# Gathering the first two expert tiles inside the routing block of a mixture-of-experts encoder

## The chip, the cores and the metric

The kernel runs on one core of a Trainium2 chip. Its time is the device time of one execution in microseconds (us), given as the median of several executions. A core has these engines: TensorE (PE, with its weight loads PEld), VectorE (DVE), ScalarE (ACT), GpSimd (POOL) and SyncE (SP). Each takes its instructions in order from its own sequencer (PEq, DVEq, ACTq, POOLq, SPq in the rows), and they meet through semaphores.

## The reference, cut to what matters

The program is one encoder layer on two sequences of 1024 tokens with 1024 features: a layer norm, a mixer (attention and a gated linear recurrence), a second norm, and then the part that the change touches, a mixture of 16 experts with two experts per token.

```python
def hier_moe(h, ...):
    xt = h.reshape(B * S, D)
    g_onehot = one_hot(argmax(xt @ router_wg + router_bg), 4)         # one of 4 groups
    e_logits_sel = einsum('tge,tg->te', xt @ router_we + router_be, g_onehot)
    top_v, top_i = top_k(e_logits_sel, 2)                             # two of its 4 experts
    top_w = softmax(top_v) * g_sel_prob
    gate = ...                                                        # (token, 16), two entries not zero
    for e in range(16):
        hid = silu(xt @ exp_w1[e]) * (xt @ exp_w3[e])                 # 1024 -> 256
        y = y + gate[:, e] * (hid @ exp_w2[e])                        # 256 -> 1024
```

The result is added to the normed input and normed once more. 2048 tokens with two experts each make 4096 pairs of token and expert, and only those are computed.

## The kernel before, in words

`build` runs six stages one after the other: `project_xy`, `qkv_lru`, `attend`, `route`, `experts` and `combine`. Each stage is a block of five programs, one per engine, with semaphores of its own. At a stage's end each engine runs a DRAIN (the row of the block's own line) and all engines meet; then POOL clears the stage's semaphores (`semaphores`, L193) and all engines drain and meet a second time. Only then does an engine start on the next stage. A context of semaphores that closes costs one such clearing and meeting.

`route` (L1725) sorts the pairs. It gives each expert a run of slots, in tiles of 128 slots, 48 tiles at most. It builds one-hot matrices: `lanes` (L1799) is a table of 128 x 32 bf16 numbers per partition, 8 KB, which ACT fills (L1869) and DVE compares with each pair's lane (L1955). 32 accumulating matmuls (L2002) then yield, for each slot, the token's number and gate. DVE turns that into row numbers, `found` (L1980 to L1983), copies them to `lists` (L1984), makes the gates (L1985 to L1987), and that is its last work of the stage. POOL makes constants at the stage's start and nothing after them. SP loads the weights of experts 0 and 1, and ACT makes the high part of expert 0's weights (L1875).

`experts` (L2006) works on tiles of 128 pairs. All products are of float32 values in three passes, high x high, high x low and low x high, so each weight has a low part, raw minus high. POOL gathers a tile's 128 rows of 4 KB from `h1_dram` into `xg[u]` by an indirect DMA (`ahead`, L2171), from a column of 128 row numbers in `ix[u]` that DVE copies out of `lists` (`index`, L2319). PE transposes the rows (`turn`, L2211), ACT makes their high part (L2291), DVE their low part (L2344), PE multiplies (`up`, L108 to L110), ACT and DVE make `hid` (L2285, L2338), PE multiplies with the second matrix (`down`), ACT scales by the gate (L2298), and POOL adds the tile's rows into `sum_dram` by an indirect DMA with an add (L2187). `run_tiles` writes out this order for every engine, with rows gathered three tiles ahead.

An expert's low parts are made by two engines. Of the four parts of the first matrix DVE makes three and POOL one (L2092, part 3); of the two parts of the second DVE makes one and POOL one (L2099). All are 128 x 1024 subtractions with both inputs in SBUF. For expert 0 this stands at the stage's start. DVE's program there begins:

```python
            index(0, 0)
            index(1, 1)
            split_first(0)
            split_rest(0)
            run_tiles(dve, skip, ahead, split_first, up, turn, skip, turn_hid, split_rest)
```

and POOL's begins:

```python
            ahead(0, 0)
            ahead(1, 1)
            split_rest(0)
            last = run_tiles(pool, skip, ahead, None, skip, skip, down, skip, split_rest)
```

PE's `up` waits for both engines' low parts of the first matrix and for the low part of the rows. SP waits for all low parts of an expert before it loads the expert after next over it (L2159, then L1720 to L1722), and only after it has issued that load does it tell ACT that the next expert's weights are ready (`w_ready`, L2155), which ACT needs before it makes their high part (L2264), still ahead of the first tile's silu (L2285).

Of the kernel before, what the change touches and what calls it, by code (L numbers as in the profile page):

```python
# [26 lines left out]
BF16 = mybir.dt.bfloat16  # L27
# [7 lines left out]
P = 128  # L35
D = 1024
# [76 lines left out]
def build(nc, x, ln_in_g, ln_in_b, w_in, conv_w, conv_b, lru_wa, lru_ba, lru_wx, lru_bx, lru_lambda,  # L113
# [13 lines left out]
    with ExitStack() as whole:  # L127
# [44 lines left out]
        with ExitStack() as kept:  # L172
            sb = lambda n, s, d=F32: kept.enter_context(nc.sbuf_tensor(n, s, d))

            up_w = [sb(n, [P, 2, KD, 2 * DE], d) for n, d in (("up_raw", F32), ("up_hi", F32R), ("up_lo", F32R))]
            down_w = [sb(n, [P, 2, KE, D], d) for n, d in (("down_raw", F32), ("down_hi", F32R), ("down_lo", F32R))]
            route(nc, ident, logits, gates, *tables, exp_w1, exp_w3, exp_w2, up_w, down_w)
            experts(nc, exp_w1, exp_w3, exp_w2, up_w, down_w, ident, gates, *tables, h1_dram, sum_dram)
        combine(nc, ln2_g[0], ln2_b[0], sum_dram, out)

# [1541 lines left out]

def route(nc, ident, logits, gates, lists, tile_expert, split_at, pair_live, last_tile,  # L1725
          exp_w1, exp_w3, exp_w2, up_w, down_w):

# [3 lines left out]
    with ExitStack() as ctx:  # L1733
# [62 lines left out]
        vals = sb("vals", [P, VALS, PAIRS], BF16)  # L1796
        part_i = sb("part_i", [P, 2, PAIRS], I32)
        part = sb("part", [P, 2, PAIRS], BF16)
        lanes = sb("lanes", [P, P, PAIRS], BF16)  # L1799
        tiles = sb("tiles", [P, MT, PAIRS], BF16)  # L1800
        hot_lane = sb("hot_lane", [P, P, PAIRS], BF16)
        hot_tile = sb("hot_tile", [P, MT, PAIRS], BF16)
# [25 lines left out]
        @block.gpsimd  # L1828
        def _(pool):
            link = Chain(pool, pool_link)  # L1830
            for j in range(G):
                pool.memset(order[:, :, j], float(G - j)).then_inc(made, 1)
            pool.memset(ones[:], 1.0).then_inc(made, 1)
            pool.memset(busy[:], 0.0).then_inc(zeroed, 1)
            link(pool.memset(tri_f[:], 0.0))

            link(pool.affine_select(out=tri_f[:], in_=tri_f[:], compare_op=ALU.is_gt, fill=-1.0, base=0,
                                    pattern=[[1, P]], channel_multiplier=-1))
            pool.tensor_copy(tri[:], tri_f[:]).then_inc(made, 1)
            link(pool.memset(from_first[:], 1.0))  # L1840
            pool.memset(from_first[:, :, 0], 0.0).then_inc(made, 1)
            link(pool.iota(thr_i[:], [[P, NT]], base=0, channel_multiplier=0))
            pool.tensor_copy(thr[:], thr_i[:]).then_inc(made, 1)
            link(pool.iota(spare_i[:], [[1, 1]], base=T + 1, channel_multiplier=1))
            pool.tensor_copy(spare[:], spare_i[:]).then_inc(made, 1)
            link(pool.iota(lane_i[:], [[1, P]], base=0, channel_multiplier=0))
            pool.tensor_copy(lane_f[:], lane_i[:]).then_inc(made, 1)
            link(pool.iota(tile_i[:], [[1, MT]], base=0, channel_multiplier=0))
            pool.tensor_copy(tile_f[:], tile_i[:]).then_inc(made, 1)
            link(pool.iota(row_i[:], [[0, NT]], base=1, channel_multiplier=1))  # L1850
            for c in range(2):
                half = slice(c * NT, (c + 1) * NT)
                pool.tensor_copy(vals[:, 0, half], tile_i[:, 0:NT]).then_inc(vals_done, 1)
                pool.tensor_copy(vals[:, 1, half], row_i[:]).then_inc(vals_done, 1)

        @block.sync
        def _(sp):
# [6 lines left out]
        def _(act):  # L1864
# [1 line left out]
            act.activation(ge[:], gd[:], ACT.Exp).then_inc(ge_done, 1)  # L1866

            act.wait_ge(made, G + 7)
            act.activation(lanes[:], lane_f[:].unsqueeze(2).broadcast_to([P, P, PAIRS]), ACT.Copy).then_inc(spread, 1)  # L1869
            act.wait_ge(gap_done, 1)  # L1870
            act.activation(x2[:], gap[:], ACT.Exp).then_inc(x2_done, 1)
            act.activation(tiles[:], tile_f[:].unsqueeze(2).broadcast_to([P, MT, PAIRS]), ACT.Copy).then_inc(spread, 1)
# [6 lines left out]
        def _(dve):  # L1879
# [101 lines left out]
            link(dve.scalar_tensor_tensor(number[:], list_ps[:, 0], float(P), found[:], ALU.mult, ALU.add))  # L1981
            link(dve.tensor_scalar(found[:], number[:], 0.5, spare[:], ALU.is_lt, ALU.mult))
            link(dve.scalar_tensor_tensor(found[:], number[:], -1.0, found[:], ALU.add, ALU.add))  # L1983
            link(dve.tensor_copy(lists[:, 0:MT], found[:]))  # L1984
            link(dve.tensor_copy(gates[:], list_ps[:, 4]))  # L1985
            link(dve.tensor_tensor(gates[:], gates[:], list_ps[:, 3], ALU.add))
# [17 lines left out]

def experts(nc, exp_w1, exp_w3, exp_w2, up_w, down_w, ident, gates, lists, tile_expert, split_at, pair_live, last_tile,  # L2006
            h1_dram, sum_dram):

# [5 lines left out]
    with ExitStack() as ctx:  # L2016
# [8 lines left out]
        DOWN_POOL = 1  # L2025
        up_raw, up_hi, up_lo = up_w
        down_raw, down_hi, down_lo = down_w
        ix = [sb(f"ix{u}", [P, 1], U32) for u in range(2)]
        xg = [sb(f"xg{u}", [P, D]) for u in range(2)]
        xt_hi = [sb(f"xt_hi{u}", [P, KD, P], F32R) for u in range(2)]  # L2030
        xt_lo = [sb(f"xt_lo{u}", [P, KD, P], F32R) for u in range(2)]
        sg = sb("sg", [P, DE])
# [9 lines left out]
        y_ps = [ps(f"y_ps{c}", [P, 512]) for c in range(2)]  # L2042

        go = sem("go")
        ix_done = sem("index_ready")
        x_in = [sem(f"rows_gathered{u}") for u in range(2)]
        w_in = [sem(f"weights_loaded{b}") for b in range(2)]
        w_ready = sem("raw_weights_ready")
        up_hi_made = sem("up_hi_made")
# [116 lines left out]
        def _(pool):  # L2166
            def ahead(j, u):

                pool.wait_ge(ix_done, j + 1)
                pool.nop(nofuse=True)  # L2170
                pool.indirect_dma_start(xg[u][:], None, h1_dram, bass.IndirectOffsetOnAxis(ix[u][:, 0:1], 0))\  # L2171
                    .then_inc(x_in[u], 16)

            def split_rest(e):
# [12 lines left out]
                pool.indirect_dma_start(sum_dram, bass.IndirectOffsetOnAxis(sx[u][:, 0:1], 0), yt[u][:], None,  # L2187
                                        compute_op=ALU.add).then_inc(y_added, 16)

            ahead(0, 0)  # L2190
            ahead(1, 1)
            split_rest(0)
            last = run_tiles(pool, skip, ahead, None, skip, skip, down, skip, split_rest)
            pool.wait_ge(y_added, 16 * last + 16)
# [113 lines left out]
        def _(dve):  # L2308
# [44 lines left out]
                dve.nop(nofuse=True)  # L2353
                dve.tensor_copy(sx[u][:], lists[:, bass.ds(j, 1)]).then_inc(gate_done, 1)

            index(0, 0)
            index(1, 1)
            split_first(0)
            split_rest(0)
            run_tiles(dve, skip, ahead, split_first, up, turn, skip, turn_hid, split_rest)  # L2360
# [232 lines left out]
```

## Time and profile before

| | us |
|---|---|
| median of 3 runs | 1680.79 (1680.5 to 1683.96) |
| the profiled execution | 1685.38 |
| its span, first to last instruction | 1683.6 |
| routing | 1143.0 to 1177.4 of the span |
| experts | 1178.4 to 1625.1 |
| combine | 1626.0 to 1683.6 |

Over the whole span PE is busy 89%, DVE 65%, ACT 54% and POOL 29%, and the mean granted clock of TensorE is 0.946 of full speed. Busy time says how long an engine had an instruction in execution, not that the instruction got on: one that is held up counts as busy too. An indirect DMA on POOL counts as busy while POOL writes its descriptors, and the data moves after that.

### The profile page before, as it was taken

How to read it: one execution, taken by the hardware profiler on the slowest of the kernel's cores; microseconds unless marked ns; L12 is line 12 of the kernel's file. 1: busy time of each engine (PE TensorE's matmuls, PEld its weight loads, DVE VectorE, ACT ScalarE, POOL GpSimd, SP SyncE). 2: the span in 40 equal slices, each digit the busy share in tenths (PEclk: the TensorE clock that was granted, in tenths of full speed). 3: DMA queues.
4: the chain of work that ended last, by engine and by line, in shares of the span. 5: the costliest groups of instructions: out<-in, count | busy, mean ns of one | idle time of the engine just before them, and what ended most of it. 6: DMA issues, size and time to landing. Idle time of an engine off the chain costs nothing. (4 is left out here: it accounts for less than half of the span.)

```text
span 1683.6 us, 29356 instructions
## 1 busy us (share of the span) xinstructions
PE 1505.2 (89%) x8921; PEld 1274.0 (76%) x8923; DVE 1101.9 (65%) x2057; ACT 904.2 (54%) x1505; POOL 496.3 (29%) x345
## 2 busy tenths in 40 slices
PE   5999989999858999999999999996799999999940
PEld 5999967777647888888888888872677788777820
DVE  7787539999968776777777777666553433444238
ACT  3444447878757555555555555532555444556323
POOL 1212125565510111111111111110445443545218
PEclk9999999999969999999999999995899999999965
DMA  8855543344242111112111111124688677796466
GB/s 275 305 211 206 180 152 132 144 168 170 100 159 69 58 57 56 61 64 71 61 57 56 56 56 57 45 95 168 227 258 256 173 219 193 217 269 159 111 185 266
DMA packets 118771, 245.02 MB, mean 146 GB/s; under 512 B 18082, under 2 KB 71330, under 8 KB 118692
## 3 DMA queue, kind: packets, MB, share of 16 engines
q1 hardware_dynamic: 88752, 156.44, 26.6%
q0 software_dynamic: 12528, 45.62, 11.5%
q10 hardware_dynamic: 17412, 41.96, 6.5%
q8 instruction: 44, 0.72, 0.2%
q14 instruction: 35, 0.29, 0.1%
HBM read 149.61 MB, written 94.37 MB: 145 GB/s over the span
## 5 line engine op out<-in xcount | busy, mean ns | idle before, releaser
L1562 DVE TENSOR_TENSOR d_probs_t_lo<-d_pt_ps,d_probs_t_hi 128x512 fp32r<-128x512 f32 x256 | 164.2, 683 | 103.4 <-ACT d_probs_t_hi L1483 102.5
L1483 ACT ACTIVATE d_probs_t_hi<-d_pt_ps 128x512 fp32r<-128x512 f32 x256 | 139.2, 596 | 152.6 <-PE d_pt_ps L1339 146.1
L1705 POOL TENSOR_TENSOR d_h_tile<-d_s_tile,d_ln_g_b 128x512 f32<-128x512 f32 x30 | 38.5, 1282 | 577.5 <-ACT d_s_tile L1501 546.7
L1540 DVE TENSOR_REDUCE d_neg_max<-d_s_ps 128x1 f32<-128x1024 f32 x128 | 155.4, 1214 | 2.7 <-PE d_s_ps L1328 2.7
L108 PE MATMUL acc<-k_hi,wl_hi 128*128 128x256 f32 x512 | 146.2, 286 | 4.4 <-DVE k_lo L518 4.4
L108 PE MATMUL e_a_ps<-up_hi,e_xt_hi 128*128 x336 | 138.7, 413 | 10.5 <-issue 6.1
L110 PE MATMUL acc<-k_hi,wl_lo 128*128 128x256 f32 x512 | 145.4, 284 | 0.0
L109 PE MATMUL acc<-k_lo,wl_hi 128*128 128x256 f32 x512 | 145.3, 284 | 0.0
L1466 ACT ACTIVATE d_probs<-d_s_ps,d_neg_max 128x1024 f32<-128x1024 f32 x128 | 143.3, 1119 | 3.6 <-DVE d_neg_max L1540 3.6
L1357 PE MATMUL d_ot_ps<-d_probs_t_hi,d_v_split 128*128 128x256 f32 x512 | 129.9, 292 | 8.8 <-DVE d_probs_t_lo L1562 6.6
L1339 PE MATMUL d_pt_ps<-ident,d_probs 128*128 128x128 f32 x1024 | 134.0, 274 | 3.3 <-ACT d_probs L1466 3.2
L109 PE MATMUL e_a_ps<-up_lo,e_xt_hi 128*128 x336 | 134.7, 401 | 0.0
L110 PE MATMUL e_a_ps<-up_hi,e_xt_lo 128*128 x336 | 134.3, 400 | 0.0
L1339 PEld LDWEIGHTS d_pt_ps<-ident,d_probs 128*128 128x128 f32 x1024 | 117.7, 141 | 13.2 <-ACT d_probs L1466 5.3
L1357 PE MATMUL d_ot_ps<-d_probs_t_lo,d_v_split 128*128 128x256 f32 x512 | 125.0, 282 | 0.0
L1327 PE MATMUL d_s_ps<-k_hi,d_q_tile 128*128 128x512 f32 (+1 forms) x256 | 113.3, 442 | 4.6 <-DMA d_q_tile<-q_dram 4.6
L2171 POOL DMA_INDIRECT e_xg<-h_dram,e_ix x45 | 45.1, 1003 | 228.7 <-ACT e_yt L2298 130.1
L1357 PEld LDWEIGHTS d_ot_ps<-d_probs_t_hi,d_v_split 128*128 128x128 f32 x512 | 97.2, 190 | 17.5 <-issue 17.5
L1328 PE MATMUL d_s_ps<-k_lo,d_q_tile 128*128 128x512 f32 (+1 forms) x256 | 102.4, 400 | 0.0
L108 PEld LDWEIGHTS acc<-k_hi,wl_hi 128*128 128x128 f32 x512 | 98.1, 192 | 5.0 <-DVE k_lo L518 4.9
L108 PE MATMUL d_m_ps<-d_wo_hi,d_m_hi 128*128 128x512 f32 x240 | 99.4, 414 | 0.0
L109 PEld LDWEIGHTS acc<-k_lo,wl_hi 128*128 128x128 f32 x512 | 98.0, 191 | 0.0
(380 smaller groups left out, 4041.6 us busy)
## 6 DMA issues: line engine op xcount, KB each, us to landing
up_raw<-in_exp_w SPq DMA_DIRECT2D x32, 1024.0 KB, 10.4
down_raw<-in_exp_w SPq DMA_DIRECT2D x16, 1024.0 KB, 12.9
h_dram<-v_all ACTq DMA_DIRECT2D x16, 512.0 KB, 3.4
ht_hi_dram<-k_hi ACTq DMA_DIRECT2D x8, 1024.0 KB, 4.3
ht_lo_dram<-k_lo ACTq DMA_DIRECT2D x8, 1024.0 KB, 6.6
q_dram<-wq_raw ACTq DMA_DIRECT2D x16, 512.0 KB, 3.0
d_q_tile<-q_dram SPq DMA_DIRECT2D x16, 512.0 KB, 3.9
d_h_tile<-h_dram SPq DMA_DIRECT2D x16, 512.0 KB, 3.2
```

Source lines behind the costliest of these rows:

```text
L108: pe.matmul(out, lhs[0], rhs[0], start=first, stop=False)
L109: pe.matmul(out, lhs[0], rhs[1], start=False, stop=False)
L110: return pe.matmul(out, lhs[1], rhs[0], start=False, stop=last)
L1327: pe.matmul(out, q_t[u][:, h, :], k_hi[:, h // GQ, keys], start=True, stop=False)
L1328: last = pe.matmul(out, q_t[u][:, h, :], k_lo[:, h // GQ, keys], start=False, stop=True)
L1339: last = pe.transpose(pt_ps[c][:, j, :], pr[h % 2][:, k * P:(k + 1) * P], ident[:])
L1357: last = pe.matmul(ot_ps[:, 0:2 * P], vs[:, s * TPS + k, h // GQ].rearrange("p c d -> p (c d)"), part[:, k].rearrange("p e t -> p (e t)"), ...
L1466: act.activation(pr[h % 2][:], s_ps[h % 2][:], ACT.Exp, bias=nm[:, u, h:h + 1], accum_out=rsum[:, u, h:h + 1]).then_inc(p_done, 1)
L1483: act.activation(pt_hi[:, c * HALF:(c + 1) * HALF, h % 2], pt_ps[c][:], ACT.Copy).then_inc(pth_done[c], 1)
L1540: dve.tensor_reduce(nm[:, u, h:h + 1], s_ps[h % 2][:], AX, ALU.max, negate=True).then_inc(nm_done, 1)
L1562: dve.tensor_tensor(pt_lo[:, part, h % 2], pt_ps[c][:], pt_hi[:, part, h % 2].bitcast(F32), ALU.subtract)\
L2171: pool.indirect_dma_start(xg[u][:], None, h1_dram, bass.IndirectOffsetOnAxis(ix[u][:, 0:1], 0))\
```

## The change

The two columns of row numbers and the two buffers of rows are now made in `build`, ahead of both stages, with the three semaphores that go with them, in a context of semaphores of their own (`g_`) around `route` and `experts`. The table `lanes` no longer has memory of its own; it lies in the memory of the two row buffers, which is 8 KB per partition as well. DVE copies the first two tiles' numbers straight from `found`, between L1983 and L1984, and POOL issues the first two gathers at the end of its program in `route`. In `experts` the two `index` calls of DVE and the two `ahead` calls of POOL at the start are gone. The gathers of later tiles are as before.

```diff
--- before.py
+++ after.py
@@ -174,8 +174,17 @@
 
             up_w = [sb(n, [P, 2, KD, 2 * DE], d) for n, d in (("up_raw", F32), ("up_hi", F32R), ("up_lo", F32R))]
             down_w = [sb(n, [P, 2, KE, D], d) for n, d in (("down_raw", F32), ("down_hi", F32R), ("down_lo", F32R))]
-            route(nc, ident, logits, gates, *tables, exp_w1, exp_w3, exp_w2, up_w, down_w)
-            experts(nc, exp_w1, exp_w3, exp_w2, up_w, down_w, ident, gates, *tables, h1_dram, sum_dram)
+            ix = [sb(f"e_ix{u}", [P, 1], U32) for u in range(2)]
+            xg_both = sb("e_xg", [P, 2, D])
+            xg = [xg_both[:, u] for u in range(2)]
+            with semaphores(nc, "g_") as sem:
+
+                ix_done = sem("index_ready")
+                x_in = [sem(f"rows_gathered{u}") for u in range(2)]
+                route(nc, ident, logits, gates, *tables, exp_w1, exp_w3, exp_w2, up_w, down_w,
+                      h1_dram, ix, xg_both, ix_done, x_in)
+                experts(nc, exp_w1, exp_w3, exp_w2, up_w, down_w, ident, gates, *tables, h1_dram, sum_dram,
+                        ix, xg, ix_done, x_in)
         combine(nc, ln2_g[0], ln2_b[0], sum_dram, out)
 
 
@@ -1723,7 +1732,7 @@
 
 
 def route(nc, ident, logits, gates, lists, tile_expert, split_at, pair_live, last_tile,
-          exp_w1, exp_w3, exp_w2, up_w, down_w):
+          exp_w1, exp_w3, exp_w2, up_w, down_w, h1_dram, ix, xg_both, ix_done, x_in):
 
 
 
@@ -1796,7 +1805,8 @@
         vals = sb("vals", [P, VALS, PAIRS], BF16)
         part_i = sb("part_i", [P, 2, PAIRS], I32)
         part = sb("part", [P, 2, PAIRS], BF16)
-        lanes = sb("lanes", [P, P, PAIRS], BF16)
+
+        lanes = xg_both[:].rearrange("p u d -> p (u d)").bitcast(BF16).rearrange("p (l i) -> p l i", l=P)
         tiles = sb("tiles", [P, MT, PAIRS], BF16)
         hot_lane = sb("hot_lane", [P, P, PAIRS], BF16)
         hot_tile = sb("hot_tile", [P, MT, PAIRS], BF16)
@@ -1852,6 +1862,10 @@
                 half = slice(c * NT, (c + 1) * NT)
                 pool.tensor_copy(vals[:, 0, half], tile_i[:, 0:NT]).then_inc(vals_done, 1)
                 pool.tensor_copy(vals[:, 1, half], row_i[:]).then_inc(vals_done, 1)
+            for u in range(2):
+                pool.wait_ge(ix_done, u + 1)
+                pool.indirect_dma_start(xg_both[:, u], None, h1_dram, bass.IndirectOffsetOnAxis(ix[u][:, 0:1], 0))\
+                    .then_inc(x_in[u], 16)
 
         @block.sync
         def _(sp):
@@ -1866,7 +1880,7 @@
             act.activation(ge[:], gd[:], ACT.Exp).then_inc(ge_done, 1)
 
             act.wait_ge(made, G + 7)
-            act.activation(lanes[:], lane_f[:].unsqueeze(2).broadcast_to([P, P, PAIRS]), ACT.Copy).then_inc(spread, 1)
+            act.activation(lanes, lane_f[:].unsqueeze(2).broadcast_to([P, P, PAIRS]), ACT.Copy).then_inc(spread, 1)
             act.wait_ge(gap_done, 1)
             act.activation(x2[:], gap[:], ACT.Exp).then_inc(x2_done, 1)
             act.activation(tiles[:], tile_f[:].unsqueeze(2).broadcast_to([P, MT, PAIRS]), ACT.Copy).then_inc(spread, 1)
@@ -1981,6 +1995,8 @@
             link(dve.scalar_tensor_tensor(number[:], list_ps[:, 0], float(P), found[:], ALU.mult, ALU.add))
             link(dve.tensor_scalar(found[:], number[:], 0.5, spare[:], ALU.is_lt, ALU.mult))
             link(dve.scalar_tensor_tensor(found[:], number[:], -1.0, found[:], ALU.add, ALU.add))
+            for u in range(2):
+                dve.tensor_copy(ix[u][:], found[:, u:u + 1]).then_inc(ix_done, 1)
             link(dve.tensor_copy(lists[:, 0:MT], found[:]))
             link(dve.tensor_copy(gates[:], list_ps[:, 4]))
             link(dve.tensor_tensor(gates[:], gates[:], list_ps[:, 3], ALU.add))
@@ -2004,7 +2020,7 @@
 
 
 def experts(nc, exp_w1, exp_w3, exp_w2, up_w, down_w, ident, gates, lists, tile_expert, split_at, pair_live, last_tile,
-            h1_dram, sum_dram):
+            h1_dram, sum_dram, ix, xg, ix_done, x_in):
 
 
 
@@ -2025,8 +2041,6 @@
         DOWN_POOL = 1
         up_raw, up_hi, up_lo = up_w
         down_raw, down_hi, down_lo = down_w
-        ix = [sb(f"ix{u}", [P, 1], U32) for u in range(2)]
-        xg = [sb(f"xg{u}", [P, D]) for u in range(2)]
         xt_hi = [sb(f"xt_hi{u}", [P, KD, P], F32R) for u in range(2)]
         xt_lo = [sb(f"xt_lo{u}", [P, KD, P], F32R) for u in range(2)]
         sg = sb("sg", [P, DE])
@@ -2042,8 +2056,6 @@
         y_ps = [ps(f"y_ps{c}", [P, 512]) for c in range(2)]
 
         go = sem("go")
-        ix_done = sem("index_ready")
-        x_in = [sem(f"rows_gathered{u}") for u in range(2)]
         w_in = [sem(f"weights_loaded{b}") for b in range(2)]
         w_ready = sem("raw_weights_ready")
         up_hi_made = sem("up_hi_made")
@@ -2168,7 +2180,7 @@
 
                 pool.wait_ge(ix_done, j + 1)
                 pool.nop(nofuse=True)
-                pool.indirect_dma_start(xg[u][:], None, h1_dram, bass.IndirectOffsetOnAxis(ix[u][:, 0:1], 0))\
+                pool.indirect_dma_start(xg[u], None, h1_dram, bass.IndirectOffsetOnAxis(ix[u][:, 0:1], 0))\
                     .then_inc(x_in[u], 16)
 
             def split_rest(e):
@@ -2187,8 +2199,6 @@
                 pool.indirect_dma_start(sum_dram, bass.IndirectOffsetOnAxis(sx[u][:, 0:1], 0), yt[u][:], None,
                                         compute_op=ALU.add).then_inc(y_added, 16)
 
-            ahead(0, 0)
-            ahead(1, 1)
             split_rest(0)
             last = run_tiles(pool, skip, ahead, None, skip, skip, down, skip, split_rest)
             pool.wait_ge(y_added, 16 * last + 16)
@@ -2353,8 +2363,6 @@
                 dve.nop(nofuse=True)
                 dve.tensor_copy(sx[u][:], lists[:, bass.ds(j, 1)]).then_inc(gate_done, 1)
 
-            index(0, 0)
-            index(1, 1)
             split_first(0)
             split_rest(0)
             run_tiles(dve, skip, ahead, split_first, up, turn, skip, turn_hid, split_rest)
```

## Rows read from the trace of the kernel before

**Rows 1.** Busy time of each engine by stretch, all times in us.

```profile
core 0: us, PE busy (x) PEld busy (x) DVE busy (x) ACT busy (x) POOL busy (x), PEclk, DMA share, GB/s
1176.00:1185.00 9.00, 0.35 (x2) 0.35 (x3) 6.03 (x12) 0.00 (x0) 4.62 (x3) 0.50 0.27 76
1188.00:1191.00 3.00, 3.00 (x9) 2.35 (x8) 0.04 (x1) 0.02 (x1) 1.20 (x2) 0.52 0.36 102
1191.00:1195.00 4.00, 4.00 (x20) 3.22 (x19) 2.64 (x3) 3.98 (x5) 0.00 (x0) 1.00 1.06 376
1216.00:1616.00 400.00, 382.35 (x1814) 308.29 (x1812) 158.56 (x333) 200.48 (x320) 177.22 (x109) 0.99 0.74 203
```

**Rows 2.** Timeline of DVE at the boundary: start, us, instruction, [idle before].

```profile
1176.29 0.21 DVE L1983 SCALAR_TENSOR_TENSOR r_found<-r_number,r_found 128x48 f32<-128x48 f32 x1
1176.53 0.19 DVE L1984 CAST lists<-r_found 128x48 uint32<-128x48 f32 x1
1177.23 0.20 DVE L1987 TENSOR_TENSOR gates<-gates,list_ps 128x48 f32<-128x48 f32 x1
1178.95 0.21 DVE L2319 COPY e_ix<-lists 128x1 uint32<-128x1 uint32 x2 [1.51 <-ACTq L2254]
1179.10 3.50 DVE L2092 TENSOR_TENSOR up_lo<-up_raw,up_hi 128x1024 fp32r<-128x1024 f32 x3
1182.51 1.22 DVE L2099 TENSOR_TENSOR down_lo<-down_raw,down_hi 128x1024 fp32r<-128x1024 f32 x1
1186.43 0.69 DVE L2344 TENSOR_TENSOR e_xt_lo<-e_t_ps,e_xt_hi 128x512 fp32r<-128x512 f32 x1 [2.71 <-ACT e_xt_hi L2291]
```

**Rows 3.** Timeline of POOL at the start of the experts.

```profile
1180.07 1.31 POOL L2171 DMA_INDIRECT e_xg<-h_dram,e_ix  x1 [32.32 <-DVE e_ix L2319]
1181.68 1.74 POOL L2171 DMA_INDIRECT e_xg<-h_dram,e_ix  x1 [0.30 <-issue]
1183.43 2.50 POOL L2092 TENSOR_TENSOR up_lo<-up_raw,up_hi 128x1024 fp32r<-128x1024 f32 x1
1185.89 2.35 POOL L2099 TENSOR_TENSOR down_lo<-down_raw,down_hi 128x1024 fp32r<-128x1024 f32 x1
```

**Rows 4.** Timelines of PE, SP and ACT in the first tile.

```profile
1184.65 1.97 PE L2211 MATMUL e_t_ps<-ident,e_xg 128*128 128x128 f32 x8 [9.24 <-DMA e_xg<-h_dram,e_ix]
1187.44 0.79 PE L108 MATMUL e_a_ps<-up_hi,e_xt_hi 128*128 x1 [0.82 <-DVE e_xt_lo L2344]
1188.48 0.39 SPq L1720 DMA_DIRECT2D up_raw<-in_exp_w  x1
1190.98 3.90 ACT L2264 ACTIVATE up_hi<-up_raw  x4 [3.72 <-SPq L2155]
1194.90 1.28 ACT L2285 ACT_TABLE_LOAD   x1
```

**Rows 5.** All gathers and scatters: count, shortest/median/longest ns, first and last start.

```profile
L2171 POOL DMA_INDIRECT e_xg<-h_dram,e_ix x45: 936/980/1737, 1180.1 to 1606.0; - x45
L2187 POOL DMA_INDIRECT sum_dram<-e_yt,e_sx x42: 1572/1593/2605, 1209.3 to 1614.8; - x42
```

**Rows 6.** Meeting of the engines at the end of routing (ns, start in us).

```profile
L1733 DVEq DRAIN  x1: 10/10/10, 1177.7 to 1177.7; - x1
L193 ACTq EVENT_SEMAPHORE  x1: 17/17/17, 1178.4 to 1178.4; - x1
```

**Rows 7.** The end of the experts on POOL, and the meetings after it.

```profile
1614.78 1.57 POOL L2187 DMA_INDIRECT sum_dram<-e_yt,e_sx  x1 [5.11 <-DMA sum_dram<-e_yt,e_sx]
L2195 POOLq EVENT_SEMAPHORE  x1: 17/17/17, 1620.7 to 1620.7; - x1
L2016 POOLq DRAIN  x1: 4030/4030/4030, 1621.1 to 1621.1; - x1
L2016 SPq EVENT_SEMAPHORE  x1: 17/17/17, 1625.2 to 1625.2; - x1
L193 SPq EVENT_SEMAPHORE  x1: 17/17/17, 1625.9 to 1625.9; - x1
```

**Rows 8.** Splits of two later experts, timelines of POOL and DVE.

```profile
1240.24 2.73 POOL L2092 TENSOR_TENSOR up_lo<-up_raw,up_hi  x1
1240.32 6.10 DVE L2099 TENSOR_TENSOR down_lo<-down_raw,down_hi  x1 [2.01 <-ACT down_hi L2273]
1242.59 2.74 POOL L2099 TENSOR_TENSOR down_lo<-down_raw,down_hi  x1
...
1413.07 1.23 DVE L2099 TENSOR_TENSOR down_lo<-down_raw,down_hi  x1 [1.60 <-ACT down_hi L2273]
1413.09 3.45 POOL L2092 TENSOR_TENSOR up_lo<-up_raw,up_hi  x1
```

## The prediction

> **What bounds the kernel now.** I read the busy time by stretch first. From 1216 to 1616 PE is busy 382.35 of 400 us at full clock [rows 1]: the stage of the experts runs at the pace of PE, in a fixed order, so whatever delays the first tile's products is not made up later, and whatever brings them forward is kept. From 1176 to 1185 PE is busy 0.35 of 9 us: a hole between two stages, and the change works in it. The timelines of DVE, POOL and PE then show what fills the hole. The row numbers are ready at 1176.50 (L1983), DVE's last result is done at 1177.43, the engines meet, and DVE's first instruction of the next stage starts at 1178.95 [rows 2]. POOL issues the two gathers from 1180.07 to 1183.42, and only then does its two subtractions, to 1188.24 [rows 3]. DVE does its four subtractions from 1179.10 to 1183.73, while POOL writes descriptors [rows 2, 3]. The first rows arrive at 1184.65, PE turns them, DVE's low part starts at 1186.43, and the first product starts at 1187.44, 1.01 us after that [rows 2, 4]. So the wait that ends last before the first product is the one for the gathered rows; the subtractions are done beneath it. The question is what ends last once the rows come early.
>
> **The gathers move.** The two copies of row numbers take 0.21 us [rows 2] and go where L1984 was, at 1176.53; DVE's tail then ends at 1177.64, which costs nothing while POOL is later. From the copies' start to the first gather's was 1180.07 - 1178.95 = 1.12 us, so POOL starts at 1176.53 + 1.12 = 1177.65. A gather takes 0.98 us where nothing slows it [rows 5] (the first two took 1.31 and 1.74 beside DVE's subtractions), with 0.30 between two [rows 3]: the second is issued by 1177.65 + 0.98 + 0.30 + 0.98 = 1179.91. The first gather's rows reached PE 3.27 us after its issue ended (1184.65 - 1181.38). The first tile's rows are thus there at 1181.9, 2.7 us earlier, and the second tile's at about 1183.2, or 1183.3 as the two transfers overlap more.
>
> **What the move puts into POOL's queue.** POOL cannot leave the routing block before its DRAIN is over, and everybody waits for POOL there. The trace has one DRAIN of POOL behind indirect DMAs, at the end of the experts. There the last scatter had landed at 1620.7, and the DRAIN still took 4.03 us from 1621.1 [rows 7]. It is no ordinary empty drain (DVE's took 0.01 us [rows 6]), so it has to do with the DMAs. Bounds: it could cost nothing and let POOL go at 1179.9; it could wait for the landing and then take 4.03 us more, to 1187.3. Between them I take that it waits for the landing and does something for each DMA issued since the last DRAIN: 45 + 42 = 87 of them [rows 5] at 4.03 / 87 = 0.046 us, so 0.1 us for two. POOL is then free at 1183.3 + 0.1 = 1183.4, where DVE was free at 1177.7 [rows 6]. The meeting and clearing take 1178.4 - 1177.7 = 0.7 us [rows 6], so the experts' stage starts at 1184.1 in place of 1178.4: 5.7 us late. The rows are there by then; the gain of 2.7 us is behind another wait.
>
> **What the late start uncovers.** DVE's first instruction came 0.55 us after the start of the stage, with five semaphore increments in front (1178.95 against 1178.4). It now is a subtraction, at 1184.65. POOL no longer has two gathers ahead of its subtractions, has fewer instructions in front than DVE, and starts them at about 1184.5. So for the first time all six subtractions of expert 0 want to run at once. Later experts show what happens then. With DVE first by 0.02 us, POOL's subtraction took 3.45 us, 1.1 more than the 2.35 of an undisturbed one [rows 3, 8]. With POOL first by 0.08 us, DVE's took 6.10 in place of 1.22: it ended 1.09 us after both of POOL's were over, which together took 1240.24 to 1245.33, 5.09 us [rows 2, 8]. They exclude each other, and the one that comes second gets nothing done. With POOL first, DVE is held to 1184.5 + 5.1 = 1189.6, and its four subtractions, 1183.73 - 1179.10 = 4.63 us in all [rows 2], end at 1194.2. The rows' low part comes behind them in DVE's queue (PE and ACT have their part of the turning done by 1187.1 or so: 1.97 and 0.6 us), and the first product starts 1.0 us later at 1195.2: 7.7 us later than 1187.44.
>
> The Trainium skill, in "SBUF — State Buffer", section "SBUF: two separate sides", says the port pair that DVE and POOL share is locked for one whole instruction by whoever starts first. By that DVE would get in after POOL's first subtraction, at 1187.0, PE could start at 1192.6, and what is late is the chain over SP below, 5.8 us. The row of 6.10 us, held across two instructions of POOL, says otherwise, and I go by the row [rows 8].
>
> The other path is SP's. It waited for POOL's last subtraction (1188.24), issued at 1188.48, and ACT's high part of expert 1 started at 1190.98, 2.74 us after POOL's end, was done at 1194.88, and the silu's table load followed at 1194.90, just as PE was ready [rows 3, 4]. Now the last subtraction ends at 1194.2 (1194.0 if DVE goes first), ACT starts at 1196.9 and ends at 1200.8: 5.9 us late and beneath the 7.7 of PE, since PE's first products, which lasted from 1187.44 to about 1194.8, now end at 1202.5.
>
> **The clock.** The granted clock stood at 0.50 in the hole and through the first products and came to full speed at about 1190.9: 3.4 us after the first product, 6.2 after the first transpose [rows 1, 4]. With 8 us of idling between transposes and products the rise comes between 3.4 and 6.2 us after the products start. The extra, 0 to 2.8 us at half speed, costs 0 to 1.3 us. I take 0.5.
>
> **The further edits.** The closing of the added context of semaphores is one more clearing and meeting between the experts and `combine`, which nothing covers since all engines stand still: 1625.9 - 1625.2 = 0.7 us by its neighbour [rows 7], 0.5 at least as only three semaphores are cleared; I take 0.6. The shared memory of `lanes` adds no wait: the last comparison with it is long over when the row numbers exist, since they follow from its products. Two `index` copies and two gathers leave the experts' stage; their 0.21 us on DVE was in the shadow. Gathers of tile 2 and later come as late as the stage, three tiles ahead of need, and cost nothing.
>
> **The sum.** 7.7 + 0.5 + 0.6 = 8.8 us. The profiled execution would take 1685.38 + 8.8 = 1694.2; it stood 4.6 above the median of the runs, so I put the sum on the median: 1680.8 + 8.8 = 1689.6.
>
> **Rivals.**
> (1) *DVE gets in first, or in between.* For: two instructions 0.15 us apart by my estimate, and in two of the shown pairs either engine was first. Then PE is held by POOL's first subtraction, and the path over SP decides: 5.8 + 0.6 = 6.4, 1687.2.
> (2) *The DRAIN takes its 4 us whatever was issued.* For: the only row there is. Against: nothing that I can read, except that there 87 DMAs were behind it. Then 8.8 + 3.9 = 12.7, 1693.5.
> (3) *The DRAIN does not wait for data.* This is the one that ends on the other side. For: the row began when all had landed, so it doesn't show that a DRAIN waits for a landing. Then POOL is free at 1179.9, everything is 3.5 us earlier: with DVE first 6.4 - 3.5 = 2.9, with POOL first 5.3; and if the subtractions did not exclude each other, DVE would be done at 1185.8, the product would start at 1186.8, 0.6 earlier than before, and the added meeting eats that: 0.0, 1680.8. It decides from a DRAIN shorter than 0.3 us. For faster than before it would need more than that, since DVE's 4.63 us stand behind the stage's start and no longer beneath a transfer.
> (4) *The DRAIN waits, but the subtractions do not collide* (POOL's start falls late): DVE is done at 1189.3, the product starts at 1190.3, 2.9 late; with 0.6 it is 3.5, 1684.3.
>
> **How the numbers follow.** A difference under 0.2%, 3.4 us, can't be told from none. I give the forecast 0.42, (1) 0.18, (2) 0.15, (3) 0.14, (4) 0.06, and 0.05 to what I don't see. Slower by over 0.2% are the forecast, (1), (2), half of (4) and the larger half of (3): 0.83. Within 0.2%: 0.12. Faster: 0.05. The range goes from 1682.8, which takes in rival (3) with DVE first, to 1694.5, which holds rival (2).
>
> **What would show it.** After: two gathers on POOL at 1177.7 and 1178.9 (shift the span's offset off by L1983), 0.98 us each; a DRAIN of POOL at the block's end of over 3 us, and its end beside the second gather's last packet; first instruction of the experts 5 to 6 us later, counted from L1983; POOL's subtractions ahead of DVE's, a first subtraction of DVE of 6 us; the first product about 7.7 us later; one more pair of drains ahead of `combine`. The reading is wrong if POOL's DRAIN is under 0.3 us, or if the first product comes no more than 3 us later.

## The result, and the profile after

The changed kernel takes 1688.07 us in the median of 10 runs (1684.91 to 1693.92), the kernel before 1679.69 (1678.49 to 1684.93, 10 runs). The ratio is 1.0047, with a 95% interval of 1.0036 to 1.0059: slower by 7.9 us, 6.0 to 9.9 (the two medians are 8.4 apart). The forecast was 8.8 us slower.

The two profiled executions hide most of this: their spans are 1683.6 and 1684.8 us. The one of before had the granted clock fall to 0.5 for a few us twice in the experts' stage, near 1250 and 1342, and was itself 5.7 us above the median of its runs. So the traces are compared over the boundary alone, and times there are counted from the start of the instruction that completes the row numbers (L1983 before, at 1176.29; L1997 after, at 1176.17):

```profile
1176.17 0.21 DVE L1997 SCALAR_TENSOR_TENSOR r_found<-r_number,r_found 128x48 f32<-128x48 f32 x1
```

The timeline of POOL after, for [rows 3]:

```profile
1176.86 1.19 POOL L1867 DMA_INDIRECT e_xg<-h_dram,e_ix  x1 [29.23 <-DVE e_ix L1999]
1178.34 0.94 POOL L1867 DMA_INDIRECT e_xg<-h_dram,e_ix  x1 [0.30 <-issue]
1184.56 2.34 POOL L2104 TENSOR_TENSOR up_lo<-up_raw,up_hi 128x1024 fp32r<-128x1024 f32 x1 [5.27 <-ACTq L2266]
1186.86 3.32 POOL L2111 TENSOR_TENSOR down_lo<-down_raw,down_hi 128x1024 fp32r<-128x1024 f32 x1
```

```profile
L1742 POOLq DRAIN  x1: 6887/6887/6887, 1176.7 to 1176.7; - x1
L1742 DVEq DRAIN  x1: 10/10/10, 1177.7 to 1177.7; - x1
```

DVE is through at 1177.7 as before, POOL's DRAIN ends at 1176.66 + 6.89 = 1183.55, and all wait for it. The row of a sequencer begins when the sequencer gets there, here before the gathers have begun, so of the 6.89 us only the 4.3 us behind their issue (1179.28 to 1183.55) are waiting alone. The gathers' last data moved at about 1182.9: this is the strip of the busy share of the DMA engines from 1176 to 1184, 40 slices of 0.2 us each.

```profile
DMA  0000000000000499659899859579866431100000
```

The timeline of DVE after, for [rows 2], and the durations (shortest/median/longest, ns) of its three instructions in the first line:

```profile
1176.41 0.22 DVE L1999 CAST e_ix<-r_found 128x1 uint32<-128x1 f32 x2
1184.90 7.50 DVE L2104 TENSOR_TENSOR up_lo<-up_raw,up_hi 128x1024 fp32r<-128x1024 f32 x3 [7.46 <-ACTq L2265]
1192.32 1.21 DVE L2111 TENSOR_TENSOR down_lo<-down_raw,down_hi 128x1024 fp32r<-128x1024 f32 x1
```

```profile
L2104 DVE TENSOR_TENSOR up_lo<-up_raw,up_hi x3: 1211/3086/3355, 1184.9 to 1191.2; 128x1024 fp32r<-128x1024 f32 x3
```

Three subtractions that took 3.50 us take 7.50: two of them stood about 2.0 us each behind POOL's, and POOL's second stood 1.0 us behind DVE's first (3.32 in place of 2.35). They take turns, one instruction each. Then PE, SP and ACT, for [rows 4]:

```profile
1186.14 1.94 PE L2221 MATMUL e_t_ps<-ident,e_xg 128*128 128x128 f32 x8 [10.85 <-issue]
1194.45 0.79 PE L108 MATMUL e_a_ps<-up_hi,e_xt_hi 128*128 x1 [6.37 <-DVE e_xt_lo L2354]
```

```profile
1193.83 0.39 SPq L1729 DMA_DIRECT2D up_raw<-in_exp_w  x1
```

```profile
1196.30 3.90 ACT L2274 ACTIVATE up_hi<-up_raw  x4 [7.59 <-SPq L2167]
1200.22 1.28 ACT L2295 ACT_TABLE_LOAD   x1
1202.36 0.39 ACT L2295 ACTIVATE e_sg<-e_a_ps 128x256 f32<-128x256 f32 x1 [0.86 <-PE e_a_ps L110]
```

The first product came 11.15 us after the row numbers and now comes 18.28 after them, 7.1 us later. The silu of the kernel before came at 1194.90 + 1.28, 19.9 after them, and now comes 26.2 after them: only 6.3 later.

```profile
1196.19 0.38 ACT L2285 ACTIVATE e_sg<-e_a_ps 128x256 f32<-128x256 f32 x1
```

The table load makes the difference. It used to lie between PE's last product and the silu; now ACT does it while PE is still multiplying. At the other end two clearings and meetings in place of one stand between the experts and `combine`, 0.4 us apart:

```profile
L202 SPq EVENT_SEMAPHORE  x2: 17/17/17, 1627.1 to 1627.5; - x2
```

### The profile page after: what moved, and what is told of

It is laid out like the page before. It is cut to its first block and busy times, and to the rows that moved or that the text cites. A ratio compares the mean times of both kernels' runs of the same rounds, so it can differ in the third digit from the quotient of the medians.

```text
span 1684.8 us, 29367 instructions
## 1 busy us (share of the span) xinstructions
PE 1502.3 (89%) x8921; PEld 1271.9 (75%) x8923; DVE 1104.0 (66%) x2057; ACT 904.0 (54%) x1505; POOL 497.1 (30%) x345
```

## Experiments

Each kernel is compared with runs of the kernel before that were made beside it on the same chip. The theory: POOL's DRAIN behind the gathers delays the stage, and the subtractions that then start together hold each other up. The table at the end of the section puts the traces side by side.

**The change once more.**

> The changed kernel once more, beside its variants. Both theories: 0.3% to 0.6% slower than before. The profile should again show a DRAIN of POOL of 6 to 7 us at the end of routing, and DVE's first subtraction of the experts held up by POOL's (over 3 us in place of 1.2).

Measured: 1689.76 us (12 runs), ratio 1.0043 [1.0028, 1.0058]. DRAIN 6.98 us; DVE's three subtractions again 1.21, 3.09 and 3.36 us. The picture repeats.

**The collision taken away.**

```diff
+            pool.wait_ge(pairs_hot, PARTS * (1 + VALS))
+            pool.wait_ge(hi_made, 2)
...
+            for w, rows in ((up_w, slice(6, 8)), (down_w, slice(1, 2))):
+                pool.tensor_tensor(w[2][:, 0, rows], w[0][:, 0, rows], w[1][:, 0, rows].bitcast(F32), ALU.subtract)...
...
             for u in range(2):
                 pool.wait_ge(ix_done, u + 1)
...
-            split_rest(0)
+            pool.sem_inc(up_lo_pool, 1)
+            pool.sem_inc(down_lo_pool, 1)
```

> The changed kernel, but POOL makes its two low parts of expert 0 inside routing, where it idles, ahead of its gathers. The DRAIN stays, the collision of the six subtractions goes. Collision theory: the stage still starts at about 1184.3, DVE's four subtractions end at 1189.5 in place of 1193.5, the first product starts at about 1190.5 in place of 1194.5, and the time is 3 to 4 us below the changed kernel, 0.15% to 0.3% above before. Rival (the late start of the stage is the whole cost, the collision hides beneath PE's own start): no difference from the changed kernel, 0.4% to 0.6% above before.

Measured: 1684.07 us, ratio 1.0005 [0.9989, 1.0020]. DVE at the start of the experts, and the first product:

```profile
1185.99 3.50 DVE L2112 TENSOR_TENSOR up_lo<-up_raw,up_hi 128x1024 fp32r<-128x1024 f32 x3 [8.34 <-ACTq L2274]
1189.41 1.22 DVE L2119 TENSOR_TENSOR down_lo<-down_raw,down_hi 128x1024 fp32r<-128x1024 f32 x1
```

```profile
1191.55 0.79 PE L108 MATMUL e_a_ps<-up_hi,e_xt_hi 128*128 x1 [2.37 <-DVE e_xt_lo L2363]
```

With the DRAIN still there (6.65 us) the four subtractions are back at 4.6 us, and the product comes 3.1 us earlier against the row numbers. The rival, by which the late start alone costs, is out. DVE starts 0.9 us later than in the changed kernel here (9.6 us after the row numbers), as POOL's first gather does not start until 1.35 us after them. The median gained 5.7 us. That is more than the boundary shows, which is 3.1 at the first product and 2.5 at the silu; where the rest comes from is open. And the early subtractions are not quite free: in routing they hold up two small instructions of DVE (1.27 and 2.33 us in place of 0.19 each), and the row numbers come 33.8 us after DVE's first instruction of routing in place of 33.3. Counting from the row numbers hides these 0.5 us, here and in the last two kernels of this section.

**The gathers put back.**

```diff
-            for u in range(2):
-                pool.wait_ge(ix_done, u + 1)
-                pool.indirect_dma_start(xg_both[:, u], None, h1_dram, ...).then_inc(x_in[u], 16)
...
+            ahead(0, 0)
+            ahead(1, 1)
             split_rest(0)
```

> The changed kernel, but POOL issues the two gathers at the start of the experts, as before; the copies of the row numbers, the shared memory and the added context of semaphores stay as changed. Theory (the gathers in front of POOL's DRAIN are the cause): the DRAIN is short, the stage starts at 1178.4, POOL need not wait for DVE's copies there and the first product comes 0.5 to 1 us earlier than in the kernel before, against 0.4 us for the added meeting: 0.0% to -0.05%, no difference that can be told. Rival (something else in the change costs: the memory of the table, the added context, the copies): 0.2% or more above before.

Measured: 1682.43 us, ratio 1.0002 [0.9985, 1.0019]. The loss goes with the gathers alone; the memory of the table, the copies and the added context cost nothing that can be told. But the small gain that I expected isn't there either:

```profile
1178.18 1.96 POOL L2179 DMA_INDIRECT e_xg<-h_dram,e_ix  x1 [31.73 <-issue]
1180.44 1.73 POOL L2179 DMA_INDIRECT e_xg<-h_dram,e_ix  x1 [0.30 <-issue]
```

The first gather starts 3.18 us after the row numbers in place of 3.78, and then takes 1.96 us in place of 1.31 beside DVE's subtractions; the first product is where it was (11.20 after the row numbers, 11.15 before). Its trace also shows that the start is neither made up nor multiplied: the first silu comes 20.5 us after the row numbers here and 26.2 in the changed kernel, 5.7 apart, and the last of the 42 silus 421.9 and 427.8 us after them, 5.9 apart.

**POOL's subtractions forced behind DVE's.**

```diff
+            pool.wait_ge(down_lo_made, DOWN_PARTS - 1)
...
             split_rest(0)
```

> The changed kernel, but POOL's subtractions of expert 0 wait until DVE has done its four. If DVE and POOL exclude each other, their nine us of subtractions take nine us in any order: DVE is done at 1189.5, POOL's first at 1191.9, its second at 1194.2, the first product starts at about 1192.2, 2 us earlier than in the changed kernel, but SP's load and with it ACT's high part of expert 1 come as late as there, so the time is the changed kernel's within 1.5 us. Rival (they would have run side by side, and the long rows only show who waited in a queue): 3 us or more slower than the changed kernel, since the order is now forced one after the other.

Measured: 1689.58 us, ratio 1.0048 [1.0031, 1.0066]; the changed kernel beside it had 1.0043. Timelines of POOL, DVE and PE:

```profile
1187.37 2.34 POOL L2104 TENSOR_TENSOR up_lo<-up_raw,up_hi 128x1024 fp32r<-128x1024 f32 x1 [10.30 <-DVE down_lo L2111]
1189.67 2.36 POOL L2111 TENSOR_TENSOR down_lo<-down_raw,down_hi 128x1024 fp32r<-128x1024 f32 x1
```

```profile
1182.52 3.50 DVE L2104 TENSOR_TENSOR up_lo<-up_raw,up_hi 128x1024 fp32r<-128x1024 f32 x3 [7.31 <-ACTq L2267]
1185.93 1.22 DVE L2111 TENSOR_TENSOR down_lo<-down_raw,down_hi 128x1024 fp32r<-128x1024 f32 x1
```

```profile
1189.92 0.79 PE L108 MATMUL e_a_ps<-up_hi,e_xt_hi 128*128 x1 [4.22 <-POOL up_lo L2104]
```

All six take 9.5 us one after the other (1182.52 to 1192.03), against 9.0 where they may overlap as they like (1184.56 to 1193.53): side by side they gained 0.5 us. The product is 2.3 us earlier than in the changed kernel, and the silu is not (26.4 after the row numbers): SP's load waits for the last subtraction, whoever makes it.

**The DRAIN taken away.** The closing of routing's block asks for no DRAIN of POOL, and both stages' semaphores are cleared together with the three added ones after the experts. So two clearings and meetings fall away besides the DRAIN.

```diff
-        sem = ctx.enter_context(semaphores(nc, "r_"))
+        sem = lambda name: joint("r_" + name)
...
-        block = ctx.enter_context(nc.Block())
+        block = ctx.enter_context(nc.Block(no_gpsimd_drain=True))
```

> The changed kernel without POOL's DRAIN at the end of routing and without the clearing of routing's semaphores there (all are cleared after the experts), so that POOL leaves routing when its second gather is issued, at 1179.3. DRAIN theory: the stage starts at about 1179.5, 4.7 us earlier than in the changed kernel; the subtractions still collide, so the first product starts at about 1189.5 in place of 1194.5: 0.1% to 0.2% above before. Rival (the engines would wait for the gathered rows at some other place anyway, or the collision grows by what the start gains): no better than the changed kernel.

Measured: 1681.97 us, ratio 1.0001 [0.9988, 1.0014]. DVE's first subtraction starts 2.4 us after the row numbers in place of 8.7, and the rows arrive 5.3 after them. The subtractions collide as before, so the product comes at 12.3. Timelines of DVE and PE:

```profile
1178.56 7.79 DVE L2104 TENSOR_TENSOR up_lo<-up_raw,up_hi 128x1024 fp32r<-128x1024 f32 x3 [1.15 <-ACTq L2265]
1186.27 1.21 DVE L2111 TENSOR_TENSOR down_lo<-down_raw,down_hi 128x1024 fp32r<-128x1024 f32 x1
```

```profile
1181.43 1.97 PE L2221 MATMUL e_t_ps<-ident,e_xg 128*128 128x128 f32 x8 [6.17 <-DMA e_xg<-h_dram,e_ix]
1188.41 0.79 PE L108 MATMUL e_a_ps<-up_hi,e_xt_hi 128*128 x1 [5.01 <-DVE e_xt_lo L2354]
```

This is a little better than the 0.1% to 0.2% above before that I expected, though the interval reaches 0.14%. Not all of the gain is the DRAIN's: a clearing and meeting takes 0.4 to 0.7 us in these traces, and two are gone.

**What a DRAIN costs by itself.** Two probes in the kernel before: extra gathers on POOL in routing, each waited for before the next, into memory that nobody reads.

```diff
+            for n in range(2):          # 8 in the other
+                pool.indirect_dma_start(probe_x[:], None, h1_dram, ...).then_inc(probed, 16)
+                pool.wait_ge(probed, 16 * n + 16)
```

> The kernel before, with two extra gathers of 128 rows into a buffer that nobody reads, issued by POOL in the idle part of routing, one after the other, each waited for. They have landed long before POOL's DRAIN at the end of routing begins. Per-DMA theory (the DRAIN does 0.046 us of work for each indirect DMA since the last one): a DRAIN of 0.1 to 0.2 us. Rival (a fixed 4 us after any indirect DMA): 4 us. Neither moves the time by more than 0.1%, as POOL is idle there.

> As the probe of two, with eight gathers. Per-DMA theory: a DRAIN of 0.35 to 0.5 us, about 0.28 more than with two. Fixed cost: 4 us in both. No cost at all once landed: under 0.1 us in both, and then the 4.03 us at the end of the experts must come from the scatters or from something else.

Measured, one execution each: the DRAIN behind two took 0.21 us, behind eight 0.70.

```profile
L1733 POOLq DRAIN  x1: 212/212/212, 1164.7 to 1164.7; - x1
```

```profile
L1733 POOLq DRAIN  x1: 702/702/702, 1186.8 to 1186.8; - x1
```

So a DRAIN with all landed costs 0.08 us for each gather and 0.05 on top. That can be read only where POOL has nothing of its own to finish, as here, where it had just waited for the landing. In the kernel before, POOL's DRAIN at the end of routing has no gather behind it and still lasts 0.69 us, to the end of POOL's last cast:

```profile
L1733 POOLq DRAIN  x1: 689/689/689, 1147.1 to 1147.1; - x1
```

```profile
1147.56 0.20 POOL L1854 CAST r_vals<-r_row_i 128x16 bf16<-128x16 int32 x1
```

The eight did not fit into POOL's idle time, against what I had written: the kernel took 1693.46 us, 12 more, for the routing ended only at 1187.5. At the end of the experts the DRAIN is 4.03 us with 45 gathers behind it and 3.86 with 43, as in the changed kernel:

```profile
L2032 POOLq DRAIN  x1: 3862/3862/3862, 1622.4 to 1622.4; - x1
```

That is 0.08 for each gather again. 45 of them make 3.7 us, which leaves 0.3 for 42 scatters with add and the rest.

**More DRAINs, to shorten the last one.**

```diff
             def ahead(j, u):
+                pool.drain()
                 pool.wait_ge(ix_done, j + 1)
```

> The kernel before, with one more DRAIN on POOL ahead of each gather, where POOL waits anyway. Per-DMA theory: each of them takes 0.1 us plus what is still in flight, the DRAIN at the end of the experts falls from 4.03 us to about 0.15, and the combine stage starts 3.9 us earlier: 0.2% to 0.25% faster than before. Rival (fixed cost per DRAIN): the last DRAIN keeps its 4 us and the 45 others take 4 us each, of which POOL has 6 to 8 us of idling to hide them: no difference, or slower where a split follows.

Measured: 1703.49 us, ratio 1.0120 [1.0105, 1.0136]. Both expectations fail. The last DRAIN does fall to 0.31 us, but the others last 6 us in the median, because each waits until the scatter just before it is issued and has landed, and POOL's next gather and scatter stand behind:

```profile
L2169 POOLq DRAIN  x45: 34/6148/9317, 1177.6 to 1620.5; - x45
```

**One DRAIN ahead of the last scatter.**

```diff
-            last = run_tiles(pool, ..., split_rest)
+            last = run_tiles(pool, ..., split_rest, before_last=pool.drain)
```

> The kernel before, with one DRAIN more on POOL, after its loop over the tiles and ahead of the last scatter. The probes gave 0.21 us for two landed gathers and 0.70 for eight, 0.08 us for each, and the runs with 43 and 45 gathers ended in 3.86 and 4.03 us. Theory (the DRAIN works off what was issued since the last one, and can do so while the scatter before the last is in flight, which the last scatter waits for anyway): the added DRAIN lasts 4 to 5 us, the last scatter starts no more than 0.3 us later, the final DRAIN falls from 4.03 to under 0.4 us, and the time is 3.4 to 3.9 us below before, -0.20% to -0.23%. Rival (the DRAIN first waits for the scatter and then takes its 4 us): the last scatter is 3.7 us later and nothing is gained.

Measured: 1681.86 us, ratio 0.9999 [0.9985, 1.0012]. The rival had it. The last DRAIN falls to 0.13 us, the added one takes 6.96:

```profile
1607.72 1.59 POOL L2189 DMA_INDIRECT sum_dram<-e_yt,e_sx  x1 [1.09 <-ACT e_yt L2300]
1618.65 1.57 POOL L2189 DMA_INDIRECT sum_dram<-e_yt,e_sx  x1 [9.33 <-issue]
```

```profile
L2139 POOLq DRAIN  x1: 6963/6963/6963, 1610.5 to 1610.5; - x1
```

The busy share of the DMA engines from 1608 to 1620, 40 slices of 0.3 us each, shows the scatter's data ending at about 1613.4; the DRAIN ends 4.1 us later, at 1617.5.

```profile
DMA  9962009488799999610000000000000000000000
```

The last two scatters are 10.9 us apart in place of 6.7. The DRAIN first waits for what is in flight and then takes its 4 us; the two don't overlap, and the 4 us are only moved.

**Both causes taken away**, early low parts of POOL and no DRAIN at the end of routing, and the same with the added DRAIN:

> The changed kernel with both causes taken away: no DRAIN of POOL and no clearing at the end of routing, and POOL's low parts of expert 0 made inside routing. Theory: stage starts at 2.0 to 2.4 us after the row numbers as in the kernel without the DRAIN, DVE is done 4.6 us later, the rows arrive at about the same moment (5.3), and the first product starts 8.0 to 8.5 us after L1983's start, against 11.15 in the kernel before: 3 to 4 us faster than before, -0.15% to -0.25%. Rival (there is a third cause in the change): not below before.

> The kernel without the DRAIN and with POOL's early low parts, and with the added DRAIN ahead of the last scatter. The two gains lie at the two ends of the experts' stage and do not meet: 3 to 4 us and 3.4 to 3.9 us, together 6.5 to 8 us below before, -0.38% to -0.48%. Rival (the order at the start is lost again in the loop): no more than the late DRAIN alone gives.

Measured: 1678.32 us, ratio 0.9983 [0.9967, 0.9998]: 2.9 us below before, and some 0.6% below the changed kernel. The second: 1679.54 us, 0.9991 [0.9978, 1.0004]; its added DRAIN brings nothing, as it did alone. The first interval only just excludes no gain and the second includes it; the traces are plainer, as the silu comes 15.8 and 16.0 us after the row numbers where it came 19.9 before. Of the gain, a clearing and meeting fewer than before has its share (0.4 to 0.7 us). The early gathers do pay once neither cause stands in their way; the rows are then what ends last again:

```profile
1184.76 1.97 PE L2230 MATMUL e_t_ps<-ident,e_xg 128*128 128x128 f32 x8 [7.22 <-DMA e_xg<-h_dram,e_ix]
1187.55 0.79 PE L108 MATMUL e_a_ps<-up_hi,e_xt_hi 128*128 x1 [0.82 <-DVE e_xt_lo L2363]
```

The traces side by side, us after the start of the instruction that completes the row numbers:

| kernel | DVE's first subtraction | first product | silu | ratio |
|---|---|---|---|---|
| before | 2.8 | 11.2 | 19.9 | 1 |
| the change | 8.7 | 18.3 | 26.2 | 1.0047 |
| collision away | 9.6 | 15.2 | 23.7 | 1.0005 |
| POOL second | 8.6 | 16.0 | 26.4 | 1.0048 |
| gathers back | 2.9 | 11.2 | 20.5 | 1.0002 |
| DRAIN away | 2.4 | 12.3 | 20.9 | 1.0001 |
| both away | 2.4 | 8.7 | 15.8 | 0.9983 |

## Why the prediction was right

- *The gathers move.* Right, and earlier than I had them: POOL starts 0.45 us after the copies' start and not 1.12. The 1.12 was taken where POOL had just come from a meeting. The second gather is issued 3.1 us after the row numbers (3.6 forecast).
- *The DRAIN.* The mechanism was right: it waits for the landing, and then needs little for two DMAs. Its end came 7.4 us after the row numbers, where 7.1 was forecast, by two errors that offset each other: issue 0.5 earlier, and from issue to the DRAIN's end 4.3 us where I had 3.4 + 0.1. I had also compared the row of 4.03 us with DVE's DRAIN alone; POOL's own in routing took 0.69 us with no DMA behind it. The price for each DMA was mis-sized, 0.046 for all 87 alike; it is 0.08 for a gather and next to nothing for a scatter. The probes exclude rival (2), the fixed 4 us, and the changed kernel excludes rival (3).
- *The late stage.* DVE's first instruction of the experts comes 8.7 us after the row numbers in place of 2.7: 6.1 later, 5.7 forecast.
- *The collision.* It is there, POOL starts first (1184.56 against 1184.90), and undoing it gives 3.1 us at the first product. But the step from the row of 6.10 us failed: DVE was held there through two of POOL's instructions, and here it gets in after each. The sign I had named, a first subtraction of DVE of 6 us, did not come; it took 3.09. The sentence of the Trainium skill that I set aside ("SBUF — State Buffer", section "SBUF: two separate sides": the shared port pair is locked for one instruction) describes this trace: 3.09, 3.36 and 3.32 us beside 1.21 and 2.34, and the same again in the second profile of the change. So DVE was done 8.6 us after its start where I had 9.5, and the product came 7.1 us later and not 7.7. It did not come out as rival (1) has it either, because POOL's second subtraction held up DVE's second.
- *The clock.* From the first product to the silu's input PE took 7.9 us in place of 7.4 (1194.45 to 1202.36, and 1187.44 to 1194.8): 0.5, as forecast, which is partly luck. With the gathers put back, where the first product follows the transposes as in the kernel before, the clock came to full speed 5.0 us after the first product and not 3.4, so this varies by as much from one execution to the next. The clock came to full speed at about 1199, 4.5 us after the first product, as the granted clock (the third number from the end) of two stretches of the changed kernel shows, for [rows 1]:

```profile
1194.00:1199.00 5.00, 4.55 (x11) 3.63 (x12) 2.11 (x5) 2.70 (x3) 0.96 (x1) 0.51 0.77 249
1199.00:1203.00 4.00, 4.00 (x23) 3.29 (x21) 2.40 (x3) 3.07 (x5) 0.00 (x0) 1.00 1.07 374
```

- *What I missed.* The table load of 1.28 us lay on the path before and no longer does: -1.3 us. I had put it beneath PE in the changed kernel but not asked what it had cost in the one before.
- *The meeting.* 0.4 us, 0.6 forecast, and below the 0.5 that I had called the least.
- *The chances.* The larger half of rival (3)'s 0.14 is at least 0.07, so my own terms give at least 0.85 for slower, not 0.83.

The sum by the traces is 7.1 + 0.5 - 1.3 + 0.4 = 6.7 us, and 7.0 in the second profile of the change, where 8.8 was forecast and 7.9 [6.0, 9.9] measured. The range and the sign held; of the terms, the collision was 0.6 too large, the meeting 0.2, and the table load, 1.3, was left out. That 8.8 lies as close to 7.9 as it does is luck: the terms as the traces show them give 6.7 to 7.0, and the 0.9 to 1.2 us between that and the runs is not explained, though the interval takes it in.

The row of 6.10 us was no stray. When POOL's subtraction starts 0.00 to 0.09 us ahead of DVE's, later in the experts, either thing happens. The profiles of all the kernels here have ten such rows with DVE held through two of POOL's instructions, 5.98 to 6.20 us, and five with the engines taking turns, 3.46 to 3.50. Two at the same expert, in the second profile of the change and in the first:

```profile
1247.26 2.65 POOL L2104 TENSOR_TENSOR up_lo<-up_raw,up_hi  x1
1247.33 6.01 DVE L2111 TENSOR_TENSOR down_lo<-down_raw,down_hi  x1 [2.00 <-ACT down_hi L2283]
```

```profile
1246.99 2.44 POOL L2104 TENSOR_TENSOR up_lo<-up_raw,up_hi  x1
1247.06 3.46 DVE L2111 TENSOR_TENSOR down_lo<-down_raw,down_hi  x1 [2.01 <-ACT down_hi L2283]
1249.33 3.45 POOL L2111 TENSOR_TENSOR down_lo<-down_raw,down_hi  x1
```

The lead of POOL was 0.07 us in both. So the rows before could not say which it would be at the boundary (there POOL led by 0.34 us, and in both profiles of the change they took turns), and the sentence of the Trainium skill on the lock leaves it open too: it says that the first to start holds the ports for its instruction, not who is next when both wait. These rows also explain a part of the spread of the runs. In the second profile of the change PE idles for 0.42 and 1.62 us after the row of 6.01, and in the kernel before for 0.41 and 1.72 us after that of 6.10, with the clock at 0.50 for the 3 us behind it; after the row of 3.46 PE has no such gap. The longer of the two in the second profile of the change:

```profile
1255.79 0.50 PE L108 MATMUL e_a_ps<-up_hi,e_xt_hi 128*128 x1 [1.62 <-issue]
```

Open: what decides between the two; the rest of the spread, 9 us among runs of the changed kernel; and whether the two undoings add up. Their gains, 0.38% and 0.42%, make 0.80% where both at once gave 0.60%. At the silu the traces say the opposite, 2.5 and 5.3 us for the one and the other and 10.4 for both. There the clock has a part: it came to full speed about 6 us after the first product in either kernel with one undoing, and 3 us after it in the one with both. The intervals are too wide to tell.

## What to carry to other kernels

Before moving a DMA of POOL to the end of a stage, look at what closes the stage: a DRAIN of POOL waits for each of its indirect DMAs to land, and all engines wait for POOL, so an early gather turns into a barrier at its landing. And ask what the moved step kept apart: the two gathers at the start had kept POOL's subtractions behind DVE's, and without them the two engines met on operands in SBUF. A version with both mended (no DRAIN there, POOL's share done in its idle time) is 0.17% faster than the kernel before [0.02%, 0.33%], where the change as it stood is 0.47% slower. It also saves a clearing and meeting.

## What the runs showed of the hardware that I had not expected

- POOL's DRAIN costs 0.08 us for each gather since the last DRAIN even if all have landed: 0.21 us for 2, 0.70 for 8, 3.86 for 43 and 4.03 for 45. Scatters with add hardly count. It waits for landings first and does this after, not meanwhile.
- An indirect gather of 128 rows of 4 KB takes POOL 0.93 to 1.23 us to issue where no DVE subtraction with both inputs in SBUF runs, and up to 1.97 beside one that had started before it, so starting it earlier there gained nothing. In the kernel without the DRAIN, where the gather started 0.24 us before the subtraction, it took 0.95.
- DVE and POOL subtractions with their inputs in SBUF exclude each other, and with POOL first by under 0.1 us DVE is held through one of POOL's instructions (3.5 us) or through two (6.0); both happen.
